# Post-norm adds moved from GpSimd to VectorE, another order of the memory stage, and a third held weight slab in two products

## What is computed

```python
mem_n = rmsnorm(mem, mem_norm)
...
kv = jnp.einsum('bmd,de->bme', mem_n, w_mem_kv)      # (256 x 1024) x (1024 x 512), for each of 2 layers
...
h = rmsnorm(x, norm_mix[l])
proj = jnp.einsum('bsd,de->bse', h, a_w_in[l])       # qm = its last 256 columns
...
y = jnp.einsum("bsc,cd->bsd", mixed, w_out[l])
h = h + _rmsnorm(y, g_post_mix[l])
f_in = _rmsnorm(h, g_pre_ffn[l])
gt = jnp.einsum("bsd,df->bsf", f_in, w_gate[l])
up = jnp.einsum("bsd,df->bsf", f_in, w_up[l])
f = jnp.einsum("bsf,fd->bsd", jax.nn.silu(gt) * up, w_down[l])
h = h + _rmsnorm(f, g_post_ffn[l])
```

## Time and profile before

| | us |
|---|---|
| median of 3 runs | 1889.54 (1888.52 to 1891.11) |
| profiled execution, its own time | 1887.41 |
| its span, first to last instruction | 1885.6 |
| PE busy | 1812.6 (96%) |
| DVE busy | 955.2 (51%) |
| ACT busy | 751.8 (40%) |
| POOL busy | 135.2 (7%) |

### The profile page before, as it was taken

The page is one execution under the profiler, slowest core; times in us unless marked ns, Lnnn a source line. Parts: engine busy times, 40 slices in busy tenths (PEclk is TensorE's granted clock), DMA queues, the critical chain, the costliest instruction groups (busy, mean ns, idle before and its releaser), DMA issues.

```text
span 1885.6 us, 21605 instructions
## 1 busy us (share of the span) xinstructions
PE 1812.6 (96%) x8477; PEld 1482.7 (79%) x8477; DVE 955.2 (51%) x1696; ACT 751.8 (40%) x1475; POOL 135.2 (7%) x169
## 2 busy tenths in 40 slices
PE   7999999999999999999999999998998799999997
PEld 5887888888887777777888888776787688888885
DVE  5666443434344667755443433599944444244345
ACT  6433342323234556645232323423756343232232
POOL 0000010101001111001010101010110000000000
PEclk9999999999999999999999999999998899999999
DMA  6222233333333111123323333222100233333321
GB/s 232 81 68 82 87 93 98 99 99 97 95 101 83 56 56 57 34 58 88 100 91 101 100 91 100 86 73 67 56 1 11 79 100 101 101 90 101 101 90 56
DMA packets 195748, 158.37 MB, mean 84 GB/s; under 512 B 5248, under 2 KB 161152, under 8 KB 195648
## 3 DMA queue, kind: packets, MB, share of 16 engines
q1 hardware_dynamic: 194240, 154.16, 27.2%
q0 software_dynamic: 400, 1.25, 0.3%
q10 hardware_dynamic: 1008, 1.59, 0.2%
HBM read 154.88 MB, written 2.10 MB: 83 GB/s over the span
## 4 chain that ended last, share of the span: by engine, by line
PE 85%; DVE 10%; ACT 3%; issue 1%; DMA 0%; ACTq 0%; DVEq 0%
PE ps L752 28%; PE ps L754 26%; PE ps L753 26%; DVE sb L2261 3%; DVE sb L1856 1%; PE ps L804 1%; PE ps L1184 1%; DVE sb L2387 1%; DVE sb L1870 0%; PE ps L1072 0%; ACT sb L1403 0%; DVE sb L2392 0%; PE ps L1078 0%; ACT sb L1390 0%; DMA sb<-in_con 0%
## 5 line engine op out<-in xcount | busy, mean ns | idle before, releaser
L752 PE MATMUL ps<-sb,sb 128*128 128x512 f32 (+3 forms) x2547 | 990.6, 391 | 20.3 <-DVE sb L1856 7.6
L754 PE MATMUL ps<-sb,sb 128*128 128x512 f32 (+3 forms) x2547 | 968.0, 382 | 0.0
L753 PE MATMUL ps<-sb,sb 128*128 128x512 f32 (+3 forms) x2547 | 967.8, 382 | 0.0
L752 PEld LDWEIGHTS ps<-sb,sb 128*128 128x128 f32 (+1 forms) x2547 | 479.7, 189 | 129.6 <-issue 19.7
L754 PEld LDWEIGHTS ps<-sb,sb 128*128 128x128 f32 (+1 forms) x2547 | 479.5, 189 | 92.4
L753 PEld LDWEIGHTS ps<-sb,sb 128*128 128x128 f32 (+1 forms) x2547 | 480.3, 190 | 85.7
L1856 DVE TENSOR_TENSOR sb<-sb,sb 128x512 fp32r<-128x512 f32 x532 | 351.1, 701 | 351.8 <-ACT sb L1382 351.0
L1382 ACT ACTIVATE sb<-sb 128x512 fp32r<-128x512 f32 x532 | 305.2, 622 | 432.2 <-PE ps L754 432.2
L2065 DVE TENSOR_TENSOR sb<-sb,sb 128x512 fp32r<-128x512 f32 x64 | 68.1, 1063 | 177.0 <-ACT sb L1525 177.0
L650 POOL TENSOR_TENSOR sb<-sb 128x512 f32<-128x512 f32 x64 | 66.9, 1045 | 793.5 <-ACT sb L1535 793.5
L1535 ACT ACTIVATE sb<-ps 128x512 f32<-128x512 f32 x64 | 38.3, 598 | 208.6 <-PE ps L754 208.6
(11 more groups left out here) (204 smaller groups left out, 1031.9 us busy)
## 6 DMA issues: line engine op xcount, KB each, us to landing
sb<-in_w_up SPq DMA_DIRECT2D x86, 512.0 KB, 3.9
sb<-in_w_down SPq DMA_DIRECT2D x86, 512.0 KB, 3.8
sb<-in_w_gate SPq DMA_DIRECT2D x22, 512.0 KB, 3.8
sb<-in_a_w_in SPq DMA_DIRECT2D x20, 512.0 KB, 3.7
sb<-in_w_in SPq DMA_DIRECT2D x20, 512.0 KB, 3.7
sb<-in_w_o SPq DMA_DIRECT2D x16, 512.0 KB, 3.8
sb<-in_w_mem_kv SPq DMA_DIRECT2D x8, 512.0 KB, 7.1
sb<-in_w_out SPq DMA_DIRECT2D x8, 512.0 KB, 3.9
```

The lines of the kernel that those rows point to most:

```text
L752: mm(ps, lh, rh, start=start, stop=False, **k)
L753: mm(ps, lh, rl, start=False, stop=False, **k)
L754: return mm(ps, ll, rh, start=False, stop=stop, **k)
```

## The change

1. **Adds.** `post(c)` leaves GpSimd's program. VectorE makes both adds of every tile, in both post-norms; the counter `post_pool` is gone, and what waited for it (`x_ready`, squares, `post_mul`, stores) waits for `post_dve`, which now counts two a tile. After the output product VectorE's order is: both products, both adds, then the next tile's sum.
2. **Memory stage.** PE transposes all eight k of the memory ahead of the first product; the transposes k = 4 to 7 of X go from `qm` into the third slab of the second memory product; `qm`'s tiles wait for the memory values of their own bank, not for all. ACT and VectorE interleave splits and drains anew: the second memory square and the root go behind the split of slab 2, the squares of X between later splits, with the last behind the split of slab 9. CT is loaded behind slab 0's high part. VectorE makes its constants later. SP issues the loads of slabs 2 and 3 ahead of X.
3. **Held slabs.** `last_strips` takes three slabs in turn for each tile: (1, 2), (0, 3), (1, 3) of the output product, and (1, 1), (0, 2), (1, 2) of the last group of down2. Each is asked for at its first tile.
4. **First gate slab.** ACT and VectorE split it right behind the post-norm, ahead of the squares and drains for the FFN, and no longer behind the first four drains.

GpSimd's other work stays, its products for the gates (L717) and for the MLPs (L650) included.

```diff
...
+    OUT = [(0, 0), (0, 1), (0, 2), (1, 0), (1, 1), (1, 2), (0, 3), (1, 3)]
+    for n, j in OUT:
...
         if job == "mix0":
             return S(f"x{t}"), 16
         if job == "pre_ffn":
-            return (S("post_pool"), t + 1) if t < 3 else (S("post_dve"), 5)
+            return S("post_dve"), 2 * t + 2
...
         for t in range(2):
             e.dma_start(MEMX[:, t, :], ins["mem"][0, 128 * t:128 * t + 128, :]).then_inc(S(f"memx{t}"), 16)
         for i, (parts, kt, n, _, _) in enumerate(slabs):
-            if i == 2:
+            if i == N_RAW:
                 for t in range(4):
                     e.dma_start(X[:, t, :], ins["x"][0, 128 * t:128 * t + 128, :]).then_inc(S(f"x{t}"), 16)
...
         for t in range(4):
-            q.wait_ge(S("post_dve"), 5 + t + 1)
+            q.wait_ge(S("post_dve"), 8 + 2 * t + 1)
             e.dma_start(out[0, 128 * t:128 * t + 128, 0:512], X[:, t, 0:512]).then_inc(S("stored"), 16)
...
-        def post(c):
-            for t in range(3):
-                q.wait_ge(S("post_v"), 8 * c + 2 * t + 2)
-                TTT(X[:, t, 512:1024], TF[:, t, 512:1024], X[:, t, 512:1024], ALU.add).then_inc(S("post_pool"), 1)
-
-        post(0)
-        q.wait_ge(S("post_dve"), 5)
         q.wait_ge(S("post_v"), 8)
         e.dma_start(GP[:, :], ins["g_post_ffn_2"].broadcast_to([128, D])).then_inc(S("gp"), 16)
-        post(1)

     def tensor_program(e):
         q = Lane(e)
...

         q.wait_ge(S("con"), 16)
         turn_first(MEMX, "mem", 2)
-        for l in range(2):
-            tile_n(CH["mem", l], Bh, Bl, turned("mem"), 2 * l, lambda t: None,
-                   turn_in_chunk(MEMX, "mem", 2) if l == 0 else no_step)
-            if l == 0:
-                q.wait_ge(S("turn_lo"), 8 * JOB["mem"] + 8)
-                turn_first(X, "mix0")
-
-        tile_n(CH["qm"], Ah, Al, turned("mix0"), 0, lambda t: q.wait_ge(S("mem_v"), 4),
-               lambda j, t, k: turn_next(X, "mix0", 4 + k) if j == 0 and t == 0 else None)
+        for k in range(4, 8):
+            turn_next(MEMX, "mem", k, 2)
+        tile_n(CH["mem", 0], Bh, Bl, turned("mem"), 0, lambda t: None)
+        turn_first(X, "mix0")
+        tile_n(CH["mem", 1], Bh, Bl, turned("mem"), 2, lambda t: None,
+               lambda j, t, k: turn_next(X, "mix0", 4 + 2 * t + k) if j == 2 else None)
+
+        tile_n(CH["qm"], Ah, Al, turned("mix0"), 0, lambda t: q.wait_ge(S("mem_v"), max(t + 1, 2)))
         q.wait_ge(S("turn_lo"), 8 * JOB["mix0"] + 8)
         spread(X, "mix0")

...
                 if t == 3:
                     m.then_inc(S("w_used"), 1)

-        def last_strips(step, done):
-
-            w = [next_slab(), next_slab()]
+        def last_strips(order, step, done):
+
+            w = []
             for t in range(4):
-                for n in range(2):
-                    m = step(w[n], n, t)
-                    m.then_inc(S("w_used") if t == 3 else S(done), 1)
+                for i, (n, j) in enumerate(order):
+                    if t == 0:
+                        w.append(next_slab())
+                    m = step(w[i], j, n, t)
+                    if t == 3:
+                        m.then_inc(S("w_used"), 1)
+                    elif i > 0:
+                        m.then_inc(S(done), 1)

         held.clear()
         for step in PLAN_C:
             block_step(*step)
         q.wait_ge(S("pair_n"), 4)
         q.wait_ge(S("keep"), 8)
-        for n, j in ((0, 1), (0, 2), (1, 0), (1, 1), (1, 2)):
+        for n, j in OUT[1:5]:
             w = next_slab()
             for t in range(4):
                 m = out_strip(w, j, n, t)
             m.then_inc(S("w_used"), 1)
-        last_strips(lambda w, n, t: out_strip(w, 3, n, t), "o_tile")
+        last_strips(OUT[5:], out_strip, "o_tile")


         for k, ts in ((0, (0, 1, 2)), (1, (0, 1, 2)), (2, (0, 1, 2)), (0, (3,)), (1, (3,)), (2, (3,)), (3, (0, 1, 2, 3))):
...
             if g == 0:
                 q.wait_ge(S("turn_lo"), 8 * JOB["pre_ffn"] + 8)
                 q.wait_ge(S("spread"), 3)
-            for n, j in ((1, 0), (1, 1), (1, 2), (1, 3)) if g < 2 else ((0, 0), (0, 1), (1, 0), (1, 1)):
+            for n, j in ((1, 0), (1, 1), (1, 2), (1, 3)) if g < 2 else DN[:3]:
                 w = next_slab()
                 for t in range(4):
                     m = down_strip(w, j, n, t)
                 m.then_inc(S("w_used"), 1)
-        last_strips(lambda w, n, t: down_strip(w, 2, n, t), "d_tile")
+        last_strips(DN[3:], down_strip, "d_tile")

     def scalar_program(e):
         q = Lane(e)
...
-        for t in range(2):
-            square(MEMX, "mem", t)
-        rsqrt("mem", 2)
+        square(MEMX, "mem", 0)
         for k in range(4):
             turn("mem", Bh, "mem", k, 2)
         weights(1)
-        for k in range(4, 8):
-            turn("mem", Bh, "mem", k, 2)
-        for l in range(2):
-            c = CH["mem", l]
-            for j in range(4):
-                weights(c.first + j + 2)
-                if l == 1 and j == 0:
-                    for k in range(4):
-                        turn("mix0", Ah, "mix0", k)
-                if l == 1:
-                    square(X, "mix0", j)
-            weights(c.last + 3)
+        e.dma_start(CT[:, :], ins["con"][:, 320:832]).then_inc(S("con2"), 16)
+        for j in range(2):
+            for k in (4 + 2 * j, 5 + 2 * j):
+                turn("mem", Bh, "mem", k, 2)
+            weights(j + 2)
+        square(MEMX, "mem", 1)
+        rsqrt("mem", 2)
+
+        def mem_out(l):
             for t in range(2):
-                q.wait_ge(*tile_of(c, t))
+                q.wait_ge(*tile_of(CH["mem", l], t))
                 q.wait_ge(S("rs_n"), 3 * USE["mem"] + 3)
                 r = rms("mem", t, 1)
                 act(KS[:, l, t, :], banks[2 * l + t][:, 0:256], ACT.Copy, scale=r).then_inc(S("ks"), 1)
                 act(VMh[l][:, t, :], banks[2 * l + t][:, 256:512], ACT.Copy, scale=r).then_inc(S("mem_v_hi"), 1)
-        rsqrt("mix0", 4)
-
+
+        for j in range(3):
+            weights(j + 4)
+            square(X, "mix0", j)
+        mem_out(0)
+        weights(7)
+        for k in range(4):
+            turn("mix0", Ah, "mix0", k)
+        weights(8)
         for k in range(4, 8):
             turn("mix0", Ah, "mix0", k)
+        weights(9)
+        mem_out(1)
+        weights(10)
+        square(X, "mix0", 3)
+        rsqrt("mix0", 4)
+
...
                 q.wait_ge(*strip_done("out", n, t))
                 f_square(0, n, t, banks[4 * n + t][:, :])
             rsqrt(("post", 0, t), 1)
+        weights(SL["gt", 0] + 1)
         for t in range(2):
             square(X, "pre_ffn", t)
         for k in range(4):
...
             f_square(1, 1, t, banks[4 + t][:, :])
             rsqrt(("post", 1, t), 1)
         for t in range(4):
-            if t < 3:
-                q.wait_ge(S("post_pool"), 3 + t + 1)
-            else:
-                q.wait_ge(S("post_dve"), 10)
+            q.wait_ge(S("post_dve"), 8 + 2 * t + 2)
...
                    M[:, 6:8].unsqueeze(2).broadcast_to([128, 2, 64]), ALU.mult).then_inc(S(p + "out"), 1)


-        q.wait_ge(S("sq"), 2)
-        rsqrt_a("mem", sums("mem", 2), 2, 1.0 / D, EPS)
-        q.wait_ge(S("con"), 16)
-        q.wait_ge(S("con2"), 16)
-        e.tensor_copy(IDB[:, :], CON[:, 0:128]).then_inc(S("bits"), 1)
-        rsqrt_b("mem", rms("mem", 0, 2), 2)
         q.wait_ge(S("col"), 16)
         for k in range(4):
             turn("mem", Bh, Bl, "mem", k, 2)
         weights(1)
-        for k in range(4, 8):
-            turn("mem", Bh, Bl, "mem", k, 2)
+        for j in range(2):
+            for k in (4 + 2 * j, 5 + 2 * j):
+                turn("mem", Bh, Bl, "mem", k, 2)
+            weights(j + 2)
+        stats("mem", 2)
+
+        def mem_out(l):
+            for t in range(2):
+                q.wait_ge(S("mem_v_hi"), 2 * l + t + 1)
+                stt(VMl[l][:, t, :], banks[2 * l + t][:, 256:512], rms("mem", t, 1), VMh[l][:, t, :].bitcast(F32),
+                    ALU.mult, ALU.subtract).then_inc(S("mem_v"), 1)
+
+        weights(4)
+        q.wait_ge(S("con"), 16)
+        q.wait_ge(S("con2"), 16)
+        e.tensor_copy(IDB[:, :], CON[:, 0:128]).then_inc(S("bits"), 1)
...
+        weights(5)
...
-        for l in range(2):
-            c = CH["mem", l]
-            for j in range(4):
-                weights(c.first + j + 2)
-                if l == 1 and j == 0:
-                    for k in range(4):
-                        turn("mix0", Ah, Al, "mix0", k)
-            weights(c.last + 3)
-            for t in range(2):
-                q.wait_ge(S("mem_v_hi"), 2 * l + t + 1)
-                stt(VMl[l][:, t, :], banks[2 * l + t][:, 256:512], rms("mem", t, 1), VMh[l][:, t, :].bitcast(F32),
-                    ALU.mult, ALU.subtract).then_inc(S("mem_v"), 1)
-        stats("mix0")
+        weights(6)
+        mem_out(0)
+        weights(7)
+        for k in range(4):
```

(29 more changed lines are left out.)

## The result

The changed kernel takes 1867.87 us as the median of 4 runs (1867.42 to 1870.30), beside 1889.24 us (1888.52 to 1891.11) for the kernel before. The ratio is 0.9888, with a 95% interval of 0.9871 to 0.9905: 21.4 us less, where 20.3 were forecast. The profiled execution, 1870.3 us with a span of 1868.5, is the slowest of the four.

The account below looks back on a forecast made before the run. TensorE, busy 1365.87 of 1400 us, bounds the middle; only memory stage, turnaround and tail change. 8.9 + 8.4 + 3.0 = 20.3 us off the profiled 1887.41 gives 1867.1, as a median 1869; range 1864 to 1877.

Parts of the forecast that it names:

- Memory stage: Start of the kernel: earlier splits and transposes bring the gates' first matmul from 58.90 to 50.0 us, 8.9 us less.
- The fourth term: Memory stage: PE restarts slow once instead of twice, 8 slow matmuls instead of 17, 1.8 us less.
- Rival B: Memory stage does not run through, slab 0 or turns late: 4 us gained instead of 8.9, 1874 us; chance 0.12.
- Turnaround: From output product to gated FFN: held slab, early gate split and first tile together give 8.4 us, bounds 5 to 10.
- E: As a time: end of a product's last strip. As a rival: PE stays slow after the turnaround, 1895 us; chance 0.02.
- the clock: Turnaround, first FFN tile: PE probably restarts slow for longer than 2.7 us, so 0.6 us is taken off the gain.
- Rival A: Turnaround: ACT's queue takes over, 2 us late at two places, gain there 4.5 us, 1873 us; chance 0.14.
- End: Tail after the last matmul: the last add moves from E + 10.6 to E + 7.6, 3.0 us less, bounds 2 and 3.5.
- The held slab's margin of 0.57 us: Both last products: the third slab's split takes 2.15 us, its first strip is 2.72 us away, so PE need not wait.
- rival C: The held slab comes late in both products, 1 us each, and tiles bunch again: 1872 to 1874 us; chance 0.05.
- The adds: Turnaround: add on VectorE costs 0.60 us, blocked operation costs 1.15, so 0.55 gained for each of three tiles.
- Rival D: GpSimd's gate products are not in the diff; if the gain hung on them, time stays within 0.2%; chance 0.03.

Follow-up runs that it names:

- p1: The kernel before with only the memory stage of the change added: 1879.52 us, ratio 0.9947 to before.
- u4: The changed kernel with the three held slabs all asked for at the start, not each at its first tile: 1875.16 us, ratio 0.9922 to before.
- b2: b1 with 15 filler matmuls, whose results nobody reads, in PE's two waits of the turnaround: 1867.33 us, ratio 0.9885 to before.
- u1: The changed kernel with two held slabs instead of three in both products: 1874.96 us, ratio 0.9921 to before.
- p2: The kernel before with only the three held slabs in both last products added: 1884.55 us, ratio 0.9978 to before.
- p3: The kernel before with only the six GpSimd adds moved to VectorE, in the changed kernel's order: 1888.49 us, ratio 0.9994 to before.
- b1: The changed kernel with VectorE's second last sum moved behind tile 0's first product: 1869.35 us, ratio 0.9893 to before.
- u2: The changed kernel with the six adds back on GpSimd and VectorE in its old order: 1870.78 us, ratio 0.9897 to before.

## Why the forecast held, step by step

**Memory stage, 8.9 us forecast.** 58.66 - 49.73 = 8.9 between the means of the columns, 8.35 between the two profiled executions, 9.8 by the medians of p1. Its steps: first drain forecast at 6.97, measured 7.15; slab 0 at 8.4, measured 8.59; PE at 10.6, measured 10.64; no wait over 1 us, none. The fourth term, one slow restart in place of two, is the one with scatter: 10 slow steps after 10.64 in this profile, where 8 were forecast, 5 in p1 and 3 in u4, whose gates start 1.5 us sooner. Rival B, that the stage doesn't run through, fell.

**Turnaround, 8.4 us forecast, 8.1 measured** (24.86 - 16.76). The last tile was to be ready at E + 4.8: its last add ends at 1490.98 + 1.28 = 1492.26, E + 4.8. The first drain was forecast at E + 5.34 and came at E + 5.23, PE's start at E + 6.8 and came at E + 6.85. The tile's end was put at E + 15.8, of which 0.4 was a wait for the root, and at 16.4 with the 0.6 taken off the gain for the clock; it came at 16.76. The mis-sized term is the clock: 5.6 us at half speed (1494.31 to 1499.9) beside 2.7 before made the tile 9.91 us long and not 8.58, so it cost 1.3 us, not 0.6. The wait for the root did not show, as PE itself was later; in b2 and u4 it is about 0.2. b2 shows both halves of this: without the slow stretch the tile ends at 15.61, and then ACT's and VectorE's drains are what PE waits for. Rival A fell: ACT's queue had 0.33 us in hand where 0.2 were forecast.

How long PE stays slow after such a pause I can't say: 2.7 us before, 5.6 after, about 1.5 in u1 and 2.5 in u4, with nearly the same program. What decides it is open.

**End, 3.0 us forecast, 3.06 measured.** The sum was right, and p2 and p3 divide it as said: 2.7 for the held slab, 0.35 for the adds (0.3 forecast). VectorE's run begins with the strip that `last_sum(1)` waits for, as read. What the prediction left out is that ACT's squares follow 0.5 us behind it (b1).

**The held slab's margin of 0.57 us** held: no wait stands at the third slab in either product, and rival C fell. u4 shows how much hangs on the request at the first tile: 2.36 us for each product.

**The adds.** The forecast put 0.55 us a tile on them, 1.65 in all. That price counted the block and the add and left out the order: in p3, where VectorE is behind, 0.6 came of it, since the new order no longer covers the root's wait; in u2 2.0 came, of which 0.7 is order. That the turnaround's sum held all the same is no luck: it was built from the time behind the last strip (2.16 + 2.61 us), which has the wait in it, and not from this price. By the first half of the rule from the Trainium skill (Perfetto Trace Analysis, Optimizing Scalar/DVE Operations) the adds would have cost time on VectorE; u2 shows the reverse, as its second half, the shared read port, has it. Rival D, that the words say more than the diff, fell with the stages above, and E needed a slow clock of 43 us; the longest stretch in the changed kernel's profile is about 10 us (0.50 from 1442 to 1452).

**The median.** Forecast 1869.0, measured 1867.87; for the profiled execution 1867.1, measured 1870.3. Its three stages give 8.35 + 8.10 + 3.06 = 19.5 us, and it gives 2.4 back in between: from the first gate matmul to E 1436.91 us, 1434.55 before. A piece of that can be seen, a half-clock stretch of 3.4 us from 735.3 that the profiled execution of before has not got. Before above, after below:

```profile
730.00:745.00 15.00, 14.07 (x76) 11.20 (x75) 11.56 (x28) 7.18 (x16) 6.45 (x12) 1.00 0.21 70
```

```profile
730.00:745.00 15.00, 14.60 (x78) 11.50 (x79) 9.56 (x24) 8.32 (x21) 1.26 (x3) 0.89 0.23 71
```

The code of this part is the same in both. The 22 runs of before range over 8 us, from 1884.63 to 1892.70; the 2 us between 19.5 and 21.4 are within that, and no cause is claimed for them. The two profiled executions differ by 17.1 us. So the stages bear the forecast out, and that the medians come within 1.1 us of it is in part luck.

## What to carry to other kernels

Where a chain of short operations follows a product, look at which piece of the product arrives last and how the earlier pieces are spaced: holding one more weight slab spaced the tiles by 4.08 us, just above the 3.96 that VectorE needs, and taking it away again cost 2.7 us at each of two places (u1). Price a removed operation by the stage it stands in: by the stages the same six adds, with their order, were worth about 1 us alone (0.6 + 0.36) and 2.4 behind the held slabs (2.0 + 0.35), so single-part tests can undervalue a part; and a new order can take back what it frees, where it uncovers a wait. And list what each queue holds ahead of the operand that an idle engine waits for; a split moved past squares and drains gave 4.2 to 4.8 us by two lines.

## What the runs showed of the hardware

A VectorE operation on 128x1 with operands in SBUF lasts as long as GpSimd's add beside it, 1.26 us against 1.27 (u2), and 0.16 us without it (p3, four of four). The Trainium skill (SBUF — State Buffer, Who interferes with whom) has VectorE's second pair of ports shared with GpSimd and held by one at a time; these rows agree, and an operation of only 128x1 waits until GpSimd's whole instruction is through.

Fifteen matmuls whose results nobody reads, put into waits of 3.1 and 0.9 us, kept the granted clock at 2.4 GHz for the next 6 us (1.00 against 0.51, the 1.2 GHz level). It was worth 1.15 us in its stage beside b1 and nothing that the medians can tell.

At the start of the trace the granted clock reads 1.00 from 11 to 15 us while the matmuls step by 0.43 us: there the step is to be trusted, and not the column.
